# Hybrid decoder layer on one core: another order of steps around the recurrence gates, the mLSTM chunks and the pooling sums

## The reference, cut to what matters

```python
proj = h @ w_in                         # h: normed and modulated x
xr, gr, q, k, v, o, ig, fg, u = split(proj)
xc   = causal_dwconv(xr)                            # 4 taps
r    = sigmoid(xc @ w_a + b_a);  i = sigmoid(xc @ w_x + b_x)   # the two gates, per head
a    = exp(8 * r * log_sigmoid(lam));  b = sqrt(1 - a*a) * i * xc
hseq = scan(h = a*h + b)                            # RG-LRU
y_a  = hseq * gelu(gr)
# mLSTM, 8 chunks of 128 tokens, 4 heads of 96, state C, n, m carried from chunk to chunk
S    = (q k^T) * exp(D - m_t);  num = S v + inter * C q;  C = decay * C + (w k)^T v
y_b  = sigmoid(o) * rmsnorm(num / max(|den|, exp(-m_t)))
# pooling, windows of 2, 4, 8 and 16 tokens, one per group of 64 channels
y_c  = ((sum of the last w of u) / count - u) @ pool_w * pool_scale
x    = x + gt1 * (concat(y_a, y_b, y_c) @ w_out)
x    = x + gt2 * (relu(h2 @ w_ff1)**2 @ w_ff2)      # then a final RMSNorm
```

## Time and profile before

| what | value |
|---|---|
| median of 3 runs | 1196.27 us |
| span of the profiled execution, first to last instruction | 1193.2 us |
| its own whole time | not given apart from the span; the median lies 3.1 us above the span |
| PE busy | 1144.6 us, 96% |
| DVE, ACT, POOL busy | 59%, 36%, 26% |
| PE waits between 100 and 420 us (the mixing stage) | 13 kinds, 13.6 us in all |
| mean granted clock of PE | 0.986 |

### The profile page before, as it was taken

How to read it: one execution, slowest core, us unless ns; L and a number is a source line. 1 busy time by engine, 2 the same in 40 slices (tenths; PEclk the granted TensorE clock), 3 DMA queues, 4 the chain that set the end, 5 groups by cost and what they waited for, 6 DMA issues and landing times.

```text
span 1193.2 us, 19528 instructions
## 1 busy us (share of the span) xinstructions
PE 1144.6 (96%) x7381; PEld 1096.3 (92%) x7381; DVE 705.4 (59%) x1253; ACT 428.6 (36%) x716; POOL 305.6 (26%) x263
## 2 busy tenths in 40 slices
PE   4899999999989999999999999999999999999997
PEld 1698888889879999899999999999999999999996
DVE  4561355688775344786655655655745656656646
ACT  5542365464554353641321321411321311412431
POOL 0431101110535366761210210210210210200352
PEclk9799999999989999999999999999999999999998
DMA  8813433667344712121121120120210211111104
GB/s 304 315 65 110 124 107 124 200 176 229 121 113 137 243 54 71 37 71 37 36 72 36 54 69 21 53 70 18 59 64 19 69 53 35 53 53 36 36 1 143
DMA packets 61702, 109.87 MB, mean 92 GB/s; under 512 B 6434, under 2 KB 30278, under 8 KB 61254
## 3 DMA queue, kind: packets, MB, share of 16 engines
q1 hardware_dynamic: 51430, 84.88, 21.5%
q10 hardware_dynamic: 10208, 24.12, 6.5%
HBM read 96.81 MB, written 12.18 MB: 91 GB/s over the span
## 4 chain that ended last, share of the span: by engine, by line
PE 81%; DVE 10%; ACT 3%; DMA 3%; issue 1%; POOL 1%; SPq 1%; POOLq 0%; DVEq 0%; ACTq 0%
PE D L2298 13%; PE D L2300 13%; PE D L2299 13%; PE D L2114 6%; PE D L2116 6%; PE D L2115 6%; PE X L2300 5%; PE X L2298 5%; PE X L2299 5%; DMA RAWW<-in_WADA 1%; PE X L2085 1%; PE X L2141 1%; PE X L2142 1%; PE X L2143 1%; PE X L2189 1%
## 5 line engine op out<-in xcount | busy, mean ns | idle before, releaser
L976 POOL TENSOR_TENSOR Y_lo<-FU,Y_hi 128x344 fp32r<-128x344 f32 (+2 forms) x120 | 123.8, 1036 | 556.4 <-ACT Y_hi L1116 554.9
L1832 DVE SCALAR_TENSOR_TENSOR X<-D,MOD,X 128x344 f32<-128x344 f32 (+1 forms) x216 | 123.8, 573 | 136.8 <-PE D L2300 113.8
L2298 PE MATMUL D<-Y_hi,W_hi 128*128 128x344 f32 x576 | 185.0, 321 | 0.0
L2299 PE MATMUL D<-Y_lo,W_hi 128*128 128x344 f32 x576 | 183.9, 319 | 0.0
L2300 PE MATMUL D<-Y_hi,W_lo 128*128 128x344 f32 x576 | 183.9, 319 | 0.0
L2114 PE MATMUL D<-H_hi,W_hi 128*128 128x344 f32 x472 | 157.9, 335 | 3.7 <-POOL H_lo L976 3.1
L2115 PE MATMUL D<-H_lo,W_hi 128*128 128x344 f32 x472 | 151.8, 322 | 0.0
L2116 PE MATMUL D<-H_hi,W_lo 128*128 128x344 f32 x472 | 151.8, 322 | 0.0
L2298 PEld LDWEIGHTS D<-Y_hi,W_hi 128*128 128x128 f32 x576 | 108.3, 188 | 1.2 <-issue 0.9
L2300 PEld LDWEIGHTS D<-Y_hi,W_lo 128*128 128x128 f32 x576 | 108.4, 188 | 0.0
L2299 PEld LDWEIGHTS D<-Y_lo,W_hi 128*128 128x128 f32 x576 | 108.1, 188 | 0.0
(11 more groups left out here) (358 smaller groups left out, 2658.0 us busy)
## 6 DMA issues: line engine op xcount, KB each, us to landing
RAWW<-in_W SPq DMA_DIRECT2D x76, 512.0 KB, 3.6
RAWW<-in_WADA ACTq DMA_DIRECT2D x28, 512.0 KB, 4.2
RAWW<-in_WADA SPq DMA_DIRECT2D x20, 512.0 KB, 8.0
RAWW<-in_W ACTq DMA_DIRECT2D x18, 512.0 KB, 3.7
X0T<-in_x SPq DMA_DIRECT2D x3, 1376.0 KB, 13.1
out_y<-OUTN SPq DMA_DIRECT2D x24, 172.0 KB
X<-in_x SPq DMA_DIRECT2D x8, 344.0 KB, 5.5
NM<-nm_d SPq DMA_DIRECT2D x8, 256.0 KB, 5.2
```

Of the source, the lines that this page charges most:

```text
L976: nc.gpsimd.tensor_tensor(lo_v, fu_v, hi_v.bitcast(F32), ALU.subtract).then_inc(lo_ready, 1)
L1832: tell(V.scalar_tensor_tensor(out=tile(X, m_x, a, a + w), in0=DB[bank][:, 0:w], scalar=tile(MOD, m_g, 0, 1), in1=tile(X, m_x, a, a + w), o ...
L2298: T.matmul(out, w_h, hi(kt), start=(kt == 0), stop=False)
L2299: T.matmul(out, w_h, lo(kt), start=False, stop=False)
```

## The change

Three steps become finer: `LRUG:t` is split into `LRUG:t:0` and `LRUG:t:1` (one per gate), the load of `NM` is taken out of `LD:c` as `LN:c`, and the last part of the second pooling sums is taken out of `POOLV:1` as `POOLW:1`. With these the list is rewritten. Every instruction stays; only places in the engines' rows change. In the order of time:

- `G1` goes behind `ADA:10:1`; `ADT:10` goes behind `D:2:1` and so directly ahead of `G2`.
- The second gate of tile 0 goes behind `D:4:1`. The gates of tiles 1 and 2 stay together.
- `ADT:16` goes behind `D:9:0`. SP loads K, Q and VB of chunk 1 before the loads of the step `SMA`.
- `AB:0` goes behind `D:9:2`. `ADT:18` goes ahead of `AB:2`. `ADT:20` goes behind `D:13:0`. `ADM:21` goes ahead of `D:14:0` on DVE.
- Around `D:14:2`: `NU:6` goes ahead of `POOLV:1`, of which only the first two doublings stay there; the rest (`POOLW:1`) and `POOLS:1` go behind `HN:6`. `ADT:22`, `POOL:0:2`, `HM:6`, `ADM:22` and `POOLD:1` go behind `D:15:0`.
- `W:17` goes from the end of the stage to behind `ADT:23`.

```diff
-D:4:0 R:30 ADA:12:1 LRUG:0 R:32 LRUA:0
-D:4:1 LRUM:0
+D:4:0 R:30 ADA:12:1 LRUG:0:0 R:32
+D:4:1 LRUG:0:1 LRUA:0 LRUM:0
...
                 elif k == "LRUG":
-                    t = s[1]
...
+                    _, t, g = s
...
-                    for g in range(2):
-                        for c in range(NCH):
-                            key = (*s, g, c)
-                            done(T.matmul(take(key)[:, 0:CH], BDL[:, g * LRU_T + t, :], XC[:, c * CH:(c + 1) * CH], start=True, stop=True), key)
+                    for c in range(NCH):
+                        key = (*s, c)
+                        done(T.matmul(take(key)[:, 0:CH], BDL[:, g * LRU_T + t, :], XC[:, c * CH:(c + 1) * CH], start=True, stop=True), key)
...
                     sp.dma_start(VB[b][:].rearrange("p h v -> p (h v)"), v_d[c]).then_inc(ld_kqv[b], 16)
+                elif k == "LN":
+                    c = s[1]
                     if c >= 1:
                         sp.wait_ge(ex_ready, c)
...
-            doubled(A, U, 1, 0)
-            if j == 1:
-                doubled(B, A, 2, 0)
-                doubled(A, B, 4, 0)
-            fixed(A, 0, upper)
-            e.sem_inc(win_lower[j], 1)
-            doubled(B, A, 8 if j else 2, upper)
-            fixed(B, upper, P)
+            if 0 in parts:
+                doubled(A, U, 1, 0)
+                if j == 1:
+                    doubled(B, A, 2, 0)
+            if 1 in parts:
+                if j == 1:
+                    doubled(A, B, 4, 0)
+                fixed(A, 0, upper)
+                e.sem_inc(win_lower[j], 1)
+                doubled(B, A, 8 if j else 2, upper)
+                fixed(B, upper, P)
...
-                        pool_windows(V, 1, link)
+                        pool_windows(V, 1, link, (0,))
+                elif k == "POOLW":
+                    pool_windows(V, 1, link, (1,))
```

More of the change, by code:

```diff
@@ L123 @@
 ADA:9:0 ADA:9:1 R:23 V:6 V:7 W:3 V:8 R:25 ADT:9
-D:1:2 ADM:9 ADA:10:0 G1 ADA:10:1
-D:2:0 ADT:10 R:24
-D:2:1 ADM:10 R:26 G2
+D:1:2 ADM:9 ADA:10:0 ADA:10:1 G1
+D:2:0 R:24
+D:2:1 ADT:10 ADM:10 R:26 G2
 D:2:2 R:28 W:4 G3 ADA:11:0 R:27 R:29
@@ L135 @@
 D:5:1
-D:5:2 ADT:13 R:35 ADM:13 ADA:14:0 LRUG:1 ADA:14:1
+D:5:2 ADT:13 R:35 ADM:13 ADA:14:0 LRUG:1:0 LRUG:1:1 ADA:14:1
 D:6:0 R:37 W:7 ADT:14 LRUA:1 R:36 R:38 ADM:14
@@ L141 @@
 D:7:1 W:8 ADA:15:1 LRUC:2 R:39
-D:7:2 ADT:15 LRUG:2 LRUA:2
+D:7:2 ADT:15 LRUG:2:0 LRUG:2:1 LRUA:2
 D:8:0 R:41 ADM:15 ADA:16:0 W:9
 D:8:1 R:43
[L145 to L152, removed]
+D:8:2 R:42 ADA:16:1 R:44 W:10 LD:0 LN:0 LD:1 SMA TS TSD LRUM:2
@@ L153 @@
+D:9:0 ADT:16
+D:9:1 R:46 R:45 LN:1 ADM:16 EX:0 ADA:17:0 S:0 SX:0 ADA:17:1 W:11 R:47
+D:9:2 AB:0 ADT:17 U:0 NU:0 HN:0 CN:0 ADM:17 HM:0 EX:1 ADA:18:0 SMK S:1 SX:1 SMB:0
+D:10:0 LD:2 LN:2
+D:10:1 LD:3 LN:3 AB:1 NU:1 ADA:18:1 U:1 CN:1 HN:1
+D:10:2 HM:1 R:49 R:48 LD:4 LN:4 EX:2 W:12
+D:11:0 SMB:1 S:2 SX:2 ADT:18 AB:2 NU:2 U:2 CN:2 ADM:18 HN:2 R:50
 D:11:1 SMB:2 HM:2 R:52 EX:3 ADA:19:0 S:3 SX:3
 D:11:2 SMB:3 AB:3 ADA:19:1 W:13 LDO:0 R:51 NU:3
-D:12:0 ADT:19 U:3 HN:3 HM:3 R:53 CN:3 ADM:19 LD:5 ADA:20:0 EX:4 R:55
+D:12:0 ADT:19 U:3 HN:3 HM:3 R:53 CN:3 ADM:19 LD:5 LN:5 ADA:20:0 EX:4 R:55
@@ L156 @@
 D:12:1 S:4 SX:4 ADA:20:1 Y:0 R:54 SMC AB:4 NU:4
-D:12:2 R:56 U:4 ADT:20 HN:4 W:14 YD:0 R:58 HM:4 LD:6
-D:13:0 Y:1 ADM:20 CN:4 ADA:21:0 EX:5 YD:1 R:57
+D:12:2 R:56 U:4 HN:4 W:14 YD:0 R:58 HM:4 LD:6 LN:6
+D:13:0 ADT:20 Y:1 ADM:20 CN:4 ADA:21:0 EX:5 YD:1 R:57
 D:13:1 S:5 ADA:21:1 POOLV:0 YS POOLS:0 POOLD:0 SX:5 W:15 YSD AB:5 NU:5 HN:5 HM:5
[L160 to L164, removed]
@@ L165 @@
-D:15:0 U:6 Y:4 POOL:1:0 R:62 CN:6 POOLY:1:0 ADA:23:0 EX:7 POOL:1:1 W:16 R:64 YD:4
+D:13:2 ADT:21 R:59 U:5 CN:5 ADM:21
+D:14:0 Y:2 EX:6 YD:2
+D:14:1 ADA:22:0 S:6 SX:6 R:61 AB:6 ADA:22:1 NU:6 Y:3 POOLV:1
+D:14:2 POOL:0:0 POOL:0:1 YD:3 R:60 POOLY:0:0 POOLY:0:1 HN:6 LD:7 LN:7 POOLW:1 POOLS:1
+D:15:0 U:6 ADT:22 POOL:0:2 HM:6 ADM:22 POOLD:1 POOLY:0:2 Y:4 POOL:1:0 R:62 CN:6 POOLY:1:0 ADA:23:0 EX:7 POOL:1:1 W:16 R:64 YD:4
 D:15:1 POOLY:1:1 S:7 SX:7 POOL:1:2 POOLY:1:2 ADA:23:1 R:63
-D:15:2 Y:5 YD:5 AB:7 NU:7 ADT:23 HN:7
+D:15:2 Y:5 YD:5 AB:7 NU:7 ADT:23 W:17 HN:7
@@ L168 @@
 D:16:0 R:65 HM:7 Y:6 U:7 YD:6 CN:7 ADM:23
-D:16:1 Y:7 W:17 YD:7
+D:16:1 Y:7 YD:7
 D:16:2
@@ L222, in bank_uses @@
         elif k == "LRUG":
-            for g in range(2):
-                for c in range(NCH):
-                    add((*s, g, c), ("X0", "X1", "X2")[c])
+            for c in range(NCH):
+                add((*s, c), ("X0", "X1", "X2")[c])
         elif k == "S":
@@ L940, in u_unit, with pool_windows @@
             return N_MIX - LRU_T - POOL_T + j
-        def pool_windows(e, j, link):
+        def pool_windows(e, j, link, parts=(0, 1)):
             U, A, B = ST[u_unit(j) % 2], PA[j], PB[j]
@@ L1210, in _ @@
                 elif k == "LRUG":
-                    t = s[1]
-                    for g, (dst, bias) in enumerate(((RG, "ba"), (IG, "bx"))):
-                        for c in range(NCH):
-                            key = (*s, g, c)
-                            wait_full(act, key)
-                            nc.scalar.activation(dst[:, c * CH:(c + 1) * CH], bank(key)[:, 0:CH], ACT.Sigmoid,
-                                                 bias=col(bias, t)).then_inc(free(key), 1)
-                    for c in range(NCH):
-                        b, n = use[(*s, 1, c)]
+                    _, t, g = s
+                    dst, bias = ((RG, "ba"), (IG, "bx"))[g]
+                    for c in range(NCH):
+                        key = (*s, c)
+                        wait_full(act, key)
+                        nc.scalar.activation(dst[:, c * CH:(c + 1) * CH], bank(key)[:, 0:CH], ACT.Sigmoid,
+                                             bias=col(bias, t)).then_inc(free(key), 1)
+                    for c in range(NCH):
+                        b, n = use[(*s, c)]
                         act.wait_ge(x_free[b], n + 1)
```

## The result

The changed kernel takes 1208.68 us (median of 4 runs, 1208.11 to 1209.48) against 1196.67 for the kernel before (1195.33 to 1197.59): ratio 1.0094, 95% interval 1.0072 to 1.0116. It is slower by 12 us, where I had forecast 1198.8.

The account below looks back on a forecast made before the run. The prediction took PE's work and its waits to bound the kernel. Its terms summed to +2.5 us, which on 1196.3 gave 1198.8 us, with an own range of 1197.2 to 1200.4 and an 8-in-10 range of 1191 to 1202.

Parts of the forecast that it names:

- second gate: Tile 0: the 0.92 us wait goes, but XC of tile 1 is ready later and PE waits for it: +1.2 us.
- AB:0: Ahead of S:1: PE waits for X3 and DVE's MOD instead of a transfer, with SM stalled under a W_lo: +1.4 us.
- ADT:20: Behind D:13:0: its wait of 0.9 us goes, but Y:1 then waits 0.4 in X3 for ADM:20: -0.5 us.
- pooling: Around D:14:2: POOL:1:0 comes 1.4 us earlier, but the long wait at Y:4 costs 2.7 of low clock again: +1.3 us.
- W:17: First output product: its 1.5 us wait goes, but the W_lo delays HN:7, HM:7 and Y:7 by 0.6: -0.6 us.
- the price of a wait: Low clock in the mixing stage: one fall, behind the long wait at Y:4, 2.7 us paid in D:15:1.
- ADT:18: Ahead of AB:2: PE now waits for KW before both products, so NUM comes 0.5 us later: +0.5 us.
- G1, ADT:10, ADT:16: Two terms: small waits at G1 and ADT:10 go, net -0.4 us; ADT:16's wait is covered by D:9:0, -0.4 us.
- the first (DVE in time at `Y:4`): Rival: MOD ends before PE reaches Y:4, the clock stays up, sum -5.8 us, 1190.5 us, faster; chance 0.20.
- The third (waits only change their names): Rival: DVE sets the stage's pace, each removed wait returns in the next: 1196.3 us; chance 0.25 together with another rival.
- The fourth: Rival: POOL:1:0 at 349.9 us, clock down longer, XC with its whole stall: 1201.5 us; chance 0.10.

Follow-up runs that it names:

- fill_all: The changed kernel with extra matmuls that nobody reads ahead of seven new or longer waits of the mixing stage: 1200.99 us, ratio 1.0039.
- before_fill: The kernel before with 14 extra matmuls that nobody reads ahead of POOL:0:0: 1197.66 us, ratio 0.9994.
- pool_alone: The kernel before with only the pooling steps and D:15:0 in the new order: 1201.13 us, ratio 1.0019.
- w17_back: The changed kernel with W:17 behind Y:7 again; its own time is not given, each part undone gives back 1.3 to 2.2 us.
- ab_alone: The kernel before with only AB:0 behind D:9:2, the early loads of chunk 1 and ADT:16 behind D:9:0: 1198.73 us, ratio 1.0014.
- good_parts: The kernel before with only G1 behind ADA:10:1, ADT:10 behind D:2:1 and ADT:16 behind D:9:0: 1197.17 us, ratio 0.9998.
- experiment 3: The changed kernel with one part of the change undone at a time, in six runs; each gives back 1.3 to 2.2 us.

## Why the prediction was wrong

The sign was right and most mechanisms were, the size was not: +2.5 against +13.8 in the profiled execution. Of the miss of 11.3 us, 5.8 are the clock and 5.5 the waits: without any fall of the clock my terms give 2.5 - 2.7 = -0.2, and fill_all shows +5.3; the falls cost 13.8 - 5.3 = 8.5, where I had 2.7.

The 5.5 us of waits are spread over five terms, here without any fall of the clock, fill_all against my sum: second gate +2.2 (I had +1.2), `AB:0` +2.3 (+1.4), `ADT:20` +0.5 (-0.5), pooling -0.3 (-1.4), `W:17` +1.0 (-0.6). Even my upper bounds, which add up to +6.7 and not to the +6.9 that I wrote, stay 5 us below the measured 12.

**The step that failed: the price of a wait.** I let the clock fall once, behind the longest wait, because the trace of before shows one fall, behind 3.74 us. The waits of 1.4 and 1.5 us in that trace had no fall behind them, and I took this for a rule. It was one execution. before_fill and pool_alone walk the list of the kernel before up to `D:14:0`, and there the clock falls behind waits of 1.37 and 1.26 us in the one and of 2.13 and 1.93 in the other; in the changed kernel it did in six places. The waits vary too: `AB:0` waits 0.77 us for `EX` in the trace that I read, 1.37 and 2.13 in these two, `AB:2` 0.59, 1.90 and 1.93. So each added wait should have had a chance of 0.9 to 1.7 us on top where the low stretch lasts 3.4 us, and of up to 2.9 where it lasts 6.8 (6.68 instead of 3.74 at the gates in w17_back). Most of the loss lies at the short waits (6.3 of 7.7 us by the medians). The Trainium skill, "TensorE: Matmul & The Clock Gate", section "HAM oscillation — how this bites in real kernels", which I had weighed for the pooling alone, says that a long wait lets the clock fall each time anew; the runs agree for the long ones, since the clock fell behind or in all 13 unfilled waits of 3.7 to 5.8 us in the traces, and show falls for waits of 0.8 to 2.4 us as well, there sometimes and not each time.

**The second gate (+1.2, was +3.9).** The mechanism was right: PE came at 172.95 (I said 172.9) and waited 2.43 us. The stall of 2.25 us that I counted as gone by 1.0 did not go, it moved from `XC` to another small product:

```profile
166.42 2.18 DVE L1680 TENSOR_TENSOR T<-AG,COLS 128x8 f32<-128x8 f32 x1
175.09 0.23 DVE L1659 SCALAR_TENSOR_TENSOR XC<-XS,COLS,XC 128x8 f32<-128x8 f32 x1
...
175.38 5.43 PE L2193 MATMUL X<-XC,BDL 128*128 128x344 f32 x12 [2.43 <-DVE XC L1659]
```

The wait alone is +2.2 in fill_all, my upper bound; the clock adds 5.43 - 3.74 = 1.7.

**AB:0 and the loads (+1.4, was +3.9).** `S:1` waited for `MOD` and `SM` was stalled under the `W_lo` (1.14 us), as forecast. What I missed stands first:

```profile
236.34 0.69 DVE L1703 TENSOR_TENSOR EX<-NM,COL 128x512 f32<-128x512 f32 x1 [2.99 <-DMA NM<-nm_d]
241.80 1.14 DVE L1725 SCALAR_TENSOR_TENSOR SM<-NUM 128x4 f32<-128x4 f32 x1
246.34 0.18 DVE L1535 TENSOR_TENSOR MOD<-X,COLS 128x18 f32<-128x18 f32 x1
...
244.37 0.64 PE L2090 MATMUL X<-RAWW,CTX 128*32 128x256 f32 x8 [2.14 <-DMA RAWW<-in_WADA]
246.66 0.87 PE L2209 MATMUL X<-IDN,K 96*128 96x96 f32 x4 [1.66 <-DVE MOD L1535]
```

K, Q and VB of chunk 1 are now issued right behind `NM` of chunk 0. DVE's wait for `NM`, 1.41 us before the change, is 2.99 here and 3.18 in ab_alone, so the row up to `MOD` starts later than I had it. The 1.41 was a low value: the six other traces with the old order of loads have 1.8 to 2.5, the ten with the early loads 2.8 to 3.4. I had counted what the loads delay behind them, not what they may take from the transfer in front. That the early loads are what holds `NM` up was not tested apart from `AB:0`. The wait for `RAWW` lies inside the one for `MOD` and adds no time.

**ADT:18 (+0.5, was +1.6).** The wait of 0.83 us for `KW` is there; fill_all has +0.7, the rest is clock, behind the shortest wait of all. **ADT:20 (-0.5, was +2.0).** The 1.6 us at `D:13:0` were gained. Then `Y:1` waits 0.43 for `MOD`, as forecast, and `YS` 1.26 for `KW`, which I had not looked at:

```profile
270.87 0.58 PE L2104 MATMUL X<-SEL,ADS 128*128 128x9 f32 x4 [0.83 <-DVE KW L1710]
...
310.33 0.52 PE L2247 MATMUL X<-IDN,HM 128*128 128x128 f32 x3 [0.43 <-DVE MOD L1535]
...
318.47 0.32 PE L2253 MATMUL X<-IDN,HS 8*128 8x8 f32 x3 [1.26 <-DVE KW L1710]
```

**The pooling (+1.3, was +2.0).** The best of the terms, in part by luck: without the clock it is -0.3 and not -1.4 (fill_all), and the clock took 2.3 and not 2.7. PE waited 5.81 us at `Y:4` (I had 5.1), with `HN:6` under a `Y_lo` (1.08 and 1.17 us for 0.56 each) and the `FU` waiting for ACT, as written:

```profile
348.80 1.08 DVE L1730 TENSOR_TENSOR HM<-NUM,SM 128x384 f32<-128x384 f32 x1
349.91 1.17 DVE L1731 TENSOR_TENSOR T<-HM 128x384 f32<-128x384 f32 x1
...
356.36 0.52 DVE L1688 TENSOR_TENSOR FU<-GT,HS 128x344 f32<-128x344 f32 x1 [1.24 <-ACT GT L1211]
...
357.72 0.18 DVE L1535 TENSOR_TENSOR MOD<-X,COLS 128x18 f32<-128x18 f32 x1
...
358.04 0.88 PE L2247 MATMUL X<-IDN,HM 128*128 128x128 f32 x3 [5.81 <-DVE MOD L1535]
359.59 1.52 PE L2260 MATMUL X<-ST,BDP 128*128 128x344 f32 x2 [0.68 <-DVE ST L1785]
```

**W:17 (-0.6, was +2.2).** The 1.5 us at the output product went. The `W_lo` came 0.1 us ahead of a product of 4 columns and held it for its whole length (2.33 us, shown above). I had put it over `HM<-NUM,SM` at a cost of 0.6 and kept -1.5 to 0 as bounds, though the row of 1.27 us had shown the same stall. The upper bound should have been above zero. The stall reaches PE here:

```profile
387.25 0.52 PE L2247 MATMUL X<-IDN,HM 128*128 128x128 f32 x3 [1.95 <-DVEq L1759]
```

**G1, ADT:10, ADT:16.** -0.4 and -0.4 forecast; ADT:16 gave 0.7 to 0.8. The start of the table lies between -1.4 and +0.8 us in ten traces whose kernels are the same up to there, so the first is not told; good_parts measured no change for both.

Of the rivals, the first (DVE in time at `Y:4`) is excluded by the wait of 5.81. The third (waits only change their names) holds for part of experiment 3, where undoing a part gave back less than its place had cost. The fourth had the right direction. None had more than one fall of the clock, so the range ended 7 us too low.
